# The first block's output projection as three fp32r products, with the low parts of two weight tiles made by GpSimd

## The chip, the cores and the metric

The program runs on one NeuronCore of a Trainium2 chip. The metric is the time of one execution on the device, in microseconds. The times here are the kernel's own: 1169.44 us is the median of three runs (1168.6 to 1170.05). A profile of one further execution gives the rows below.

## The reference, cut to what matters

Two stacks of two layers each work on 256 tokens of width 1024. Of a layer of the first stack, this is what lies around the change:

```python
merged = (gates[:, :, 0] * (y_ret.astype(x.dtype) @ p_ret[l])
          + gates[:, :, 1] * (y_fox.astype(x.dtype) @ p_fox[l])
          + gates[:, :, 2] * (y_rwkv.astype(x.dtype) @ p_rwkv[l]))
x = x + merged @ w_out[l]
h = _rmsnorm(x, ffn_norm[l])
gu = h @ w_gate_up[l]
g, u = jnp.split(gu, 2, axis=-1)
x = x + (jax.nn.silu(g) * u) @ w_down[l]
```

The change is in `merged @ w_out[l]`: a 256x1024 by 1024x1024 product in float32, once in each of the two layers of the first stack. The second stack has its own output projection, which is not touched.

## The kernel before, in words

Five engines run five programs written out by hand, which meet in semaphores (`Signal`). There is no scheduler: on each engine the order is that of the code. Activations lie transposed, features over the 128 partitions and 256 tokens along the free axis. Weights come as tiles of 128x2048 float32 (1 MB) into a ring of six slots. SyncE issues these loads in a fixed order, each after the wait that frees its slot. `SLOT1` says which slot tile n of a layer uses; tiles 26 to 29 are the four tiles q = 0 to 3 of `w_out`, 256 of its rows each.

A product that is to be exact enough is made in one of two ways. Either TensorE gets the float32 tiles as they are, and the trace then shows two MATMUL rows for each matmul of the program, or weight and activation are split: a high part, rounded to fp32r by a ScalarE copy (`ACT.Copy`), and a low part, the difference, by VectorE; the helper `passes` then gives three fp32r products, high by high, high by low and low by high, which add up in PSUM. The input projections (`group`, `fill`) and the FFN (`gate_up`, `down`) go the second way, the branch products (`merge`) and the output projection (`project`) the first.

The stretch around the change, once in a layer:

- `fill` finishes the input projection. TensorE solves the second half of the RWKV recurrence (`rt_chunk_terms`, `rt_state`, `rt_output`) and does blocks 0 to 3 of `merge` in between. ScalarE copies the results out of PSUM, VectorE makes the state (`state`, `state_step`).
- VectorE normalises the last output (`centre`, `head_sums`), GpSimd makes the inverse root (`inverse_root`), and VectorE ends with `normed(1)` and `finished(1)`, four operations of 128x256. TensorE meanwhile does merge blocks 4 to 6, then turns that output (`y_transposes`, after `y_ready`), and goes on with blocks 7 to 11.
- VectorE's `merged(n)` multiplies block n by its gate and adds it up: one operation that reads PSUM, then one with both inputs in SBUF. The last four write `mT`, the merged activations. Block n of `merge` waits for `merged(n - 4)`, since they share a bank.
- `project` runs over two pairs of tiles (q0 = 0, then 2), inside over the 8 output blocks m (bank m), inside that over the tiles of the pair and k = 0, 1: 64 matmuls of 128x256. In the second half each block m releases VectorE, which adds it to x.
- `ffn` starts. VectorE has to have made the low parts of the first gate and up tiles and of the normalised x. The loads of the second iteration's tiles wait for `wo_half` (first half of `project`) and `wo` (its end).

GpSimd does nothing else in this stretch than the `inverse_root` calls.

## Time and profile before

| | |
|---|---|
| median of three runs | 1169.44 us |
| the profiled execution | 1169.03 us |
| its span | 1167.2 us |
| granted TensorE clock, mean | 0.998 |
| ScalarE and VectorE, share of the span | 43%, 64% |
| GpSimd, share of the span | 5% |
| DMA, mean | 161 GB/s |

The span runs from the first to the last record of the profile; the time of the execution is 1.83 us longer. Busy time is given for each engine apart: PE is TensorE's matmul side, PEld its weight loads, which overlap, DVE is VectorE, ACT ScalarE, POOL GpSimd and SP SyncE. The page's slices show TensorE busy nine tenths or more of nearly the whole span, and the granted clock in the top tenth in all of them.

### The profile page before, as it was taken

The numbers are of one execution on the slowest core, as the hardware profiler recorded it, in microseconds if no ns is written. First come the engines' busy times: TensorE is split into PE (matmuls) and PEld (weight loads), VectorE is DVE, ScalarE is ACT, GpSimd is POOL, SyncE is SP. The second block draws the span as 40 slices with busy tenths as digits, with TensorE's granted clock in tenths as the row PEclk, the third lists the DMA queues.
The fourth block names the chain that finished last, engine by engine and source line by source line (L and its number), as shares of the span: only waits on it lengthen the run. The fifth ranks groups of instructions, "written<-read, shape, count | busy, mean of one in ns | idle before, by whom it ended". The sixth has DMA issues, their size and how long they took to land. (4 is left out here: it accounts for less than half of the span.)

```text
span 1167.2 us, 21650 instructions
## 1 busy us (share of the span) xinstructions
PE 1136.5 (97%) x9272; PEld 1018.4 (87%) x9272; DVE 744.3 (64%) x1090; ACT 505.2 (43%) x716; POOL 55.5 (5%) x47
## 2 busy tenths in 40 slices
PE   5999999999999999999999999999999999999997
PEld 4789998899999998799998899999997777877776
DVE  5587665736665565787675556555667675567744
ACT  5355442234333344455442143333355655446642
POOL 1002000000000000011000000000002100030000
PEclk9999999999999999999999999999999999999999
DMA  9543334454454355443335345434436334353310
GB/s 350 224 161 109 122 111 161 188 201 159 182 216 174 152 195 188 147 142 109 120 106 227 124 187 217 197 147 195 180 139 227 108 109 181 112 219 132 130 65 37
DMA packets 27465, 188.15 MB, mean 161 GB/s; under 512 B 3456, under 2 KB 4352, under 8 KB 5504
## 3 DMA queue, kind: packets, MB, share of 16 engines
q1 hardware_dynamic: 25808, 175.89, 40.8%
q10 hardware_dynamic: 1440, 8.55, 1.9%
q0 software_dynamic: 144, 2.66, 0.6%
q8 instruction: 55, 0.90, 0.3%
q14 instruction: 18, 0.15, 0.0%
HBM read 181.84 MB, written 5.24 MB: 160 GB/s over the span
## 5 line engine op out<-in xcount | busy, mean ns | idle before, releaser
L650 PE MATMUL bank<-in_low,h_high 128*128 128x512 f32 x352 | 138.4, 393 | 0.0
L650 PE MATMUL bank<-in_high,h_high 128*128 128x512 f32 x288 | 117.2, 407 | 13.4 <-DVE in_low L1932 12.1
L1069 PE MATMUL bank<-h_high,gate_split 128*128 128x256 f32 x704 | 129.1, 281 | 0.2
L1069 PE MATMUL bank<-h_high,up_split 128*128 128x256 f32 x704 | 128.6, 280 | 0.0
L1085 PE MATMUL bank<-act_split,down_split 128*128 128x256 f32 x960 | 118.4, 283 | 0.0
L1085 PEld LDWEIGHTS bank<-act_split,down_split 128*128 128x128 f32 x960 | 116.6, 192 | 0.0
L675 PE MATMUL bank<-h_high,in_high 128*128 128x256 f32 x384 | 115.7, 301 | 0.5 <-DVE in_low L1806 0.5
L1357 ACT ACTIVATE in_high<-ring 128x2048 fp32r<-128x2048 f32 x47 | 89.6, 1910 | 55.3 <-PE bank L650 54.7
L650 PE MATMUL bank<-in_high,x_low 128*128 128x512 f32 x288 | 113.3, 393 | 0.0
L1069 PEld LDWEIGHTS bank<-h_high,gate_split 128*128 128x128 f32 x704 | 109.9, 189 | 0.9 <-DVE h_low L1748 0.6
L1069 PEld LDWEIGHTS bank<-h_high,up_split 128*128 128x128 f32 x704 | 109.8, 189 | 0.0
L675 PE MATMUL bank<-x_low,in_high 128*128 128x256 f32 x384 | 108.4, 282 | 0.0
L675 PE MATMUL bank<-h_high,in_low 128*128 128x256 f32 x384 | 108.3, 282 | 0.0
L1806 DVE TENSOR_TENSOR in_low<-ring,in_high 128x2048 fp32r<-128x2048 f32 x35 | 79.9, 2289 | 35.7 <-ACT in_high L1357 35.7
L1069 PE MATMUL bank<-h_low,up_split 128*128 128x256 f32 x352 | 99.2, 282 | 0.0
L1069 PE MATMUL bank<-h_low,gate_split 128*128 128x256 f32 x352 | 99.2, 282 | 0.0
L1564 ACT ACTIVATE gate_split<-ring 128x2048 fp32r<-128x2048 f32 x24 | 46.0, 1917 | 91.7 <-PE bank L1069 72.4
L650 PEld LDWEIGHTS bank<-in_high,h_high 128*128 128x128 f32 x288 | 54.6, 190 | 27.7 <-issue 14.7
L650 PEld LDWEIGHTS bank<-in_low,h_high 128*128 128x128 f32 x352 | 66.8, 190 | 13.4 <-issue 0.5
L675 PEld LDWEIGHTS bank<-h_high,in_high 128*128 128x128 f32 x384 | 73.1, 190 | 5.7 <-issue 1.4
L2226 DVE TENSOR_TENSOR down_split<-ring,down_split 128x2048 fp32r<-128x2048 f32 x20 | 45.9, 2293 | 50.0 <-ACT down_split L1564 50.0
L675 PEld LDWEIGHTS bank<-x_low,in_high 128*128 128x128 f32 x384 | 73.3, 191 | 0.1
(339 smaller groups left out, 2252.4 us busy)
## 6 DMA issues: line engine op xcount, KB each, us to landing
ring<-w_in_dram SPq DMA_DIRECT2D x72, 1024.0 KB, 4.9
ring<-w_gate_up_dram SPq DMA_DIRECT2D x44, 1024.0 KB, 7.4
ring<-w_down_dram SPq DMA_DIRECT2D x22, 1024.0 KB, 4.8
ring<-w_out_dram SPq DMA_DIRECT2D x16, 1024.0 KB, 6.0
ring<-p_all_dram SPq DMA_DIRECT2D x6, 1024.0 KB, 4.8
x_kept<-scratch ACTq DMA_DIRECT2D x4, 1024.0 KB, 4.6
x<-x_kept ACTq DMA_DIRECT2D x4, 1024.0 KB, 7.8
table<-tables_dram POOLq DMA_DIRECT2D x1, 2594.0 KB, 12.2
```

Source lines behind the costliest of these rows:

```text
L650: last = mm(bank[(n - n % 2 + t) % 4][:], a, b, start=c == 0 and i == 0, stop=c == KT - 1 and i == 2)
L675: last = mm(bank[g % 4][:, half * 256:(half + 1) * 256], a, b, start=k == 0 and i == 0, stop=k == KT - 1 and i == 2)
L1069: last = mm(bank[2 * half + part][:, f * S:(f + 1) * S], a, b, start=k == 0 and i == 0, stop=k == KT - 1 and i == 2)
L1085: last = mm(bank[4 + m // 2][:, m % 2 * S:(m % 2 + 1) * S], a, b, start=False, stop=end and m % 2 == 1 and k == 1 and i == 2)
L1357: f(in_high[n % 2][:], ring[:, n % 4, :].rearrange("p (k n) -> p k n", k=KT), ACT.Copy).then_inc(done.sem, 1)
L1564: f(w_split[part if pair is None else pair][:, 0, :], ring[:, 3 * half + part, :], ACT.Copy).then_inc(w_hi[part].sem, 1)
L1806: tt(in_low[n % 4][:], ring[:, n % 4, :].rearrange("p (k n) -> p k n", k=KT), in_high[n % 2][:].bitcast(F32), ALU.subtract).then_inc(low.s ...
L2226: tt(w[:, 1, :], ring[:, 3 * half + part, :], w[:, 0, :].bitcast(F32), ALU.subtract)\
```

## The change

Each of the 64 products of `project` becomes three in fp32r. For that, the four tiles of `w_out` and the merged activations are split.

- ScalarE makes the high parts of the weights (`out_high`): tile 0 in two halves, between the copies of the recurrence; tile 1 after `gate_tanh(l, 2)`; tile 2 after `y_copy`; tile 3 after the last merge block. It also makes the high parts of the merged activations, two 128-row groups at a time (`merged_high`).
- GpSimd makes the low parts of tiles 0 and 1, two operations of 128x1024 each (its `out_low`). Tile 0 stands before the last `inverse_root` of the layer's recurrence, tile 1 right after it.
- VectorE makes the low parts of tiles 2 and 3 and of the merged activations, behind `merged(9)` and `merged(11)`.
- The high parts lie in parts of `scratch` and in `yT`, the low parts over the tile in its ring slot, and those of the activations over `mT`.
- `project` takes the first half's blocks in the order 3 to 7, 0, 1, 2.
- The tiles of `w_out` go to slots 5, 4, 3, 2 in place of 2, 3, 4, 5. Tile 0 may then be loaded one group earlier. Of the six FFN tiles that follow, the first down tile and the second gate tile wait for the end of `project` and no longer for its middle; the second up tile and second down tile wait for the middle, but stand behind those two in SyncE's queue.
- Eight semaphores of the second stack are shared with earlier ones to make room for the new ones.

```diff
@@ -132,7 +132,7 @@
 BRANCHES = [1, 0, 2]
-SLOT1 = [n % 4 for n in range(23)] + [3, 0, 1] + [2, 3, 4, 5]
+SLOT1 = [n % 4 for n in range(23)] + [3, 0, 1] + [5, 4, 3, 2]
 SLOT2 = [n % 4 for n in range(G2)] + [1, 2, 3, 5]
@@ -192,6 +192,7 @@
         vec = sb("vec", [P, N_VEC1])
+        yT_at = -(-nc.sbuf_base // 32) * 32
         yT = sb("yT", [P, 3, 2, S])
@@ -248,6 +249,12 @@
         in_low = [nc.alloc_sbuf_tensor_at(f"in_low{i}", [P, KT, 256], F32R, offset=ring_at + 8192 * i) for i in range(4)]
+        wo_high = [nc.alloc_sbuf_tensor_at(f"out_high{q}", [P, 2, D], F32R, offset=o)
+                   for q, o in enumerate((scratch_at + 4 * 12288, scratch_at, scratch_at + 4 * 7168, yT_at))]
+        wo_low = [nc.alloc_sbuf_tensor_at(f"out_low{q}", [P, 2, D], F32R, offset=ring_at + 8192 * SLOT1[26 + q]) for q in range(4)]
+        mT_high = nc.alloc_sbuf_tensor_at("merged_high", [P, KT, S], F32R, offset=scratch_at + 4 * 5120)
+        mT_low = nc.alloc_sbuf_tensor_at("merged_low", [P, KT, S], F32R, offset=scratch_at + 4 * 2048)
 
@@ -397,6 +404,11 @@
         mg_out = sig("merge_out", 12)
+        mt_hi = sig("merged_high", 4)
+        mt_lo = sig("merged_low", 4)
+        wo_hi = sig("out_high", 5)
+        wo_lo_p = sig("out_low_pool", 4)
+        wo_lo_v = sig("out_low_vector", 2)
         wo_half = sig("wo_first_half", 1)
@@ -418,15 +430,15 @@
-        b_rot = sig("b_rot", 3)
+        b_rot = goes_on(rt_msk, 3)
...
@@ -560,7 +572,7 @@
                     load(ring_in, [g_full.after(l, 20 + i)], s, ring[:, s, :], tile(p_all[ll, b]))
-                for q, free in ((0, g_full.after(l, 23)), (3, g_full.after(l, 22)), (2, g_full.after(l, 23)), (1, mg.after(l, 4))):
+                for q, free in ((0, g_full.after(l, 22)), (1, g_full.after(l, 23)), (3, g_full.after(l, 23)), (2, mg.after(l, 4))):
                     s = SLOT1[26 + q]
@@ -574,8 +586,8 @@
 
-                ffn_loads(0, 0, [mg.after(l, 8), mg.after(l, 12), wo_half.after(l, 1)])
-                ffn_loads(1, 1, [wo_half.after(l, 1), wo.after(l, KT), wo.after(l, KT)])
+                ffn_loads(0, 0, [mg.after(l, 8), mg.after(l, 12), wo.after(l, KT)])
+                ffn_loads(1, 1, [wo.after(l, KT), wo_half.after(l, 1), wo_half.after(l, 1)])
                 with sp.Fori(0, FF_IT // 2 - 1) as j:
@@ -1036,20 +1048,21 @@
                 for q0 in (0, 2):
-                    for m in range(KT):
+                    order = [3, 4, 5, 6, 7, 0, 1, 2] if q0 == 0 else range(KT)
+                    for n, m in enumerate(order):
                         for q in (q0, q0 + 1):
-                            if m == 0:
-                                s = SLOT1[26 + q]
-                                pe.wait_ge(*ring_in[s].after(l, SLOT1[:26 + q].count(s) + 1))
-                            if q == 0 and m < 3:
-                                pe.wait_ge(*mg_out.after(l, 10 + m))
-                            w = ring[:, SLOT1[26 + q], :].rearrange("p (k n) -> p k n", k=2)
+                            if n == 0:
+                                pe.wait_ge(*(wo_lo_p.after(l, 2 * q + 2) if q < 2 else wo_lo_v.after(l, q - 1)))
+                                pe.wait_ge(*mt_lo.after(l, q + 1))
+                            if q == 0 and (m < 3 or n == 0):
+                                pe.wait_ge(*mg_out.after(l, 10 + m if m < 3 else 9))
                             for k in range(2):
-                                last = mm(bank[m][:, 0:S], w[:, k, m * P:(m + 1) * P], mT[:, 2 * q + k, :],
-                                          start=q == 0 and k == 0, stop=q == 3 and k == 1)
+                                w = [v[:, k, m * P:(m + 1) * P] for v in (wo_high[q], wo_low[q])]
+                                for i, (a, b) in enumerate(passes(w, (mT_high[:, 2 * q + k, :], mT_low[:, 2 * q + k, :]))):
+                                    last = mm(bank[m][:, 0:S], a, b, start=q == 0 and k == 0 and i == 0, stop=q == 3 and k == 1 and i == 2)
                         if q0 == 2:
                             last.then_inc(wo.sem, 1)
-                        elif m == KT - 1:
+                        elif n == KT - 1:
                             last.then_inc(wo_half.sem, 1)
@@ -1361,6 +1374,17 @@
 
+            def out_high(l, q, half=None):
+                s = SLOT1[26 + q]
+                act.wait_ge(*ring_in[s].after(l, SLOT1[:26 + q].count(s) + 1))
+                c = slice(0, 2) if half is None else slice(half, half + 1)
+                f(wo_high[q][:, c, :], ring[:, s, :].rearrange("p (k n) -> p k n", k=2)[:, c, :], ACT.Copy).then_inc(wo_hi.sem, 1)
+            def merged_high(l, f2):
+                act.wait_ge(*mg_out.after(l, 9 + f2))
+                f(mT_high[:, 2 * f2:2 * f2 + 2, :], mT[:, 2 * f2:2 * f2 + 2, :], ACT.Copy).then_inc(mt_hi.sem, 1)
             def group(l, g, split=True):
@@ -1543,10 +1567,14 @@
                     last.then_inc(rt_txc.sem, 1)
+                    if t == 1:
+                        out_high(l, 0, 0)
                     act.wait_ge(*rt_h.after(l, t + 1))
                     for c in range(2):
                         last = f(m_h[:, c], bank[4 + c][:, 0:P].rearrange("p (i v) -> p i v", i=2), ACT.Copy)
                     last.then_inc(rt_hc.sem, 1)
+                    if t == 1:
+                        out_high(l, 0, 1)
                     act.wait_ge(*rt_y.after(l, t + 1))
@@ -1554,7 +1582,15 @@
                 gate_tanh(l, 2)
+                out_high(l, 1)
                 y_copy(l, 1, y_tp, yT[:, 2], bank[4], y_T, 0.5)
+                out_high(l, 2)
+                merged_high(l, 0)
+                merged_high(l, 1)
+                act.wait_ge(*mg.after(l, 12))
+                out_high(l, 3)
+                merged_high(l, 2)
+                merged_high(l, 3)
 
@@ -2216,8 +2252,26 @@
 
-                for n in range(4, 12):
+                def merged_low(f2):
+                    dve.wait_ge(*mt_hi.after(l, f2 + 1))
+                    c = slice(2 * f2, 2 * f2 + 2)
+                    tt(mT_low[:, c, :], mT[:, c, :], mT_high[:, c, :].bitcast(F32), ALU.subtract).then_inc(mt_lo.sem, 1)
+                def out_low(q):
+                    dve.wait_ge(*wo_hi.after(l, q + 2))
+                    tt(wo_low[q][:], ring[:, SLOT1[26 + q], :].rearrange("p (k n) -> p k n", k=2), wo_high[q][:].bitcast(F32),
+                       ALU.subtract).then_inc(wo_lo_v.sem, 1)
+                for n in range(4, 10):
                     merged(n)
+                merged_low(0)
+                merged_low(1)
+                merged(10)
+                merged(11)
+                out_low(2)
+                merged_low(2)
+                out_low(3)
+                merged_low(3)
 
@@ -2441,9 +2495,19 @@
                 inverse_root(st[:, 40:48], st[:, 32:40], 1.0 / HD, 1e-5, ret_rstd)
+                def out_low(q, half, hi):
+                    pool.wait_ge(*wo_hi.after(l, hi))
+                    nc.gpsimd.tensor_tensor(wo_low[q][:, half], ring[:, SLOT1[26 + q], half * D:(half + 1) * D],
+                                            wo_high[q][:, half].bitcast(F32), ALU.subtract).then_inc(wo_lo_p.sem, 1)
                 for t in range(NT):
+                    if t == 1:
+                        out_low(0, 0, 1)
+                        out_low(0, 1, 2)
                     pool.wait_ge(*rt_ysq.after(l, t + 1))
                     inverse_root(st[:, 72 + 8 * t:76 + 8 * t], st[:, 88 + 8 * t:92 + 8 * t], 1.0 / HD, 64e-5, rt_yrs)
+                for half in range(2):
+                    out_low(1, half, 3)
                 norm(2 * l + 1)
```

How GpSimd's program reads around the last two `inverse_root` calls of a layer (each is a TENSOR_SCALAR and a TENSOR_TENSOR on `small`), before:

```order
L2424 TENSOR_SCALAR small<-small 128x4
L2426 TENSOR_TENSOR small<-small,table 128x4
L2424 TENSOR_SCALAR small<-small 128x4
L2426 TENSOR_TENSOR small<-small,table 128x4
L2424 TENSOR_SCALAR small<-small 128x2
```

And now, where `out_low_63` and `out_low_64` are the low parts of `w_out` tiles 0 and 1:

```order
L2478 TENSOR_SCALAR small<-small 128x4
L2480 TENSOR_TENSOR small<-small,table 128x4
L2500 TENSOR_TENSOR out_low_63<-ring,out_high_59 128x1024 x2
L2478 TENSOR_SCALAR small<-small 128x4
L2480 TENSOR_TENSOR small<-small,table 128x4
L2500 TENSOR_TENSOR out_low_64<-ring,out_high_60 128x1024 x2
L2478 TENSOR_SCALAR small<-small 128x2
```

Two pairs of long two-input operations have come in, one on each side of the inverse root that VectorE's `normed(1)` waits for.

VectorE's program from the end of the merge to the FFN's first low parts, before (each pair of rows is one `merged`):

```order
L2100 SCALAR_TENSOR_TENSOR scratch<-arena,bank 128x512
L2102 TENSOR_TENSOR scratch<-arena,scratch 128x512
L2100 SCALAR_TENSOR_TENSOR scratch<-arena,bank 128x512
L2102 TENSOR_TENSOR scratch<-arena,scratch 128x512
L2226 TENSOR_TENSOR gate_split<-ring,gate_split 128x2048
L2226 TENSOR_TENSOR up_split<-ring,up_split 128x2048
L2258 TENSOR_TENSOR x<-x,bank 128x256 x4
```

And now:

```order
L2136 SCALAR_TENSOR_TENSOR scratch<-arena,bank 128x512
L2138 TENSOR_TENSOR scratch<-arena,scratch 128x512
L2258 TENSOR_TENSOR merged_low<-scratch,merged_high 128x512 x2
L2136 SCALAR_TENSOR_TENSOR scratch<-arena,bank 128x512
L2138 TENSOR_TENSOR scratch<-arena,scratch 128x512
L2136 SCALAR_TENSOR_TENSOR scratch<-arena,bank 128x512
L2138 TENSOR_TENSOR scratch<-arena,scratch 128x512
L2262 TENSOR_TENSOR out_low_65<-ring,out_high_61 128x2048
L2258 TENSOR_TENSOR merged_low<-scratch,merged_high 128x512
L2262 TENSOR_TENSOR out_low_66<-ring,out_high_62 128x2048
L2258 TENSOR_TENSOR merged_low<-scratch,merged_high 128x512
L2280 TENSOR_TENSOR gate_split<-ring,gate_split 128x2048
```

Six operations stand between the old ones: two low parts of activations ahead of the last two `merged`, the other four behind them and ahead of the FFN's.

ScalarE's program from the recurrence's second half on (`scratch<-bank` are the copies `txc`, `hc` and `y` of the recurrence, `arena<-arena` is `gate_tanh`, `yT<-bank` is `y_copy`), before:

```order
L1544 ACTIVATE scratch<-bank 64x512 x2
L1548 ACTIVATE scratch<-bank 128x128 x2
L1552 ACTIVATE scratch<-bank 64x256 x2
L1392 ACTIVATE arena<-arena 128x2048
L1396 ACTIVATE yT<-bank 128x512
L1564 ACTIVATE gate_split<-ring 128x2048
```

And now:

```order
L1568 ACTIVATE scratch<-bank 64x512 x2
L1382 ACTIVATE out_high_59<-ring 128x1024
L1574 ACTIVATE scratch<-bank 128x128 x2
L1382 ACTIVATE out_high_59<-ring 128x1024
L1580 ACTIVATE scratch<-bank 64x256 x2
L1416 ACTIVATE arena<-arena 128x2048
L1382 ACTIVATE out_high_60<-ring 128x2048
L1420 ACTIVATE yT<-bank 128x512
L1382 ACTIVATE out_high_61<-ring 128x2048
L1386 ACTIVATE merged_high<-scratch 128x512 x2
L1382 ACTIVATE out_high_62<-ring 128x2048
L1386 ACTIVATE merged_high<-scratch 128x512 x2
```

The order of the old copies among themselves has stayed; nine new ones stand between and behind them.

## Rows read from the trace of the kernel before

**Rows 1.** The page's first part: busy time of each engine.

```profile
PE 1136.5 (97%) x9272; PEld 1018.4 (87%) x9272; DVE 744.3 (64%) x1090; ACT 505.2 (43%) x716; POOL 55.5 (5%) x47
```

**Rows 2.** Line L1048, first layer: min/median/max ns, first and last start.

```profile
L1048 PE MATMUL bank<-scratch,ring x128: 379/379/379, 224.4 to 251.8; 128*128 128x256 f32 x128
```

**Rows 3.** Windows, L1069 alone: stretch, length, PE and PEld busy (rows), clock, DMA.

```profile
266.12:271.79 5.67, 5.65 (x48) 5.65 (x48) 1.00 0.00 0
```

**Rows 4.** Timeline, 209 to 216 us: start, length, engine, line, idle before.

```profile
209.49 1.91 ACT L1392 ACTIVATE arena<-arena 128x2048 f32<-128x2048 f32 x1 [0.25 <-DVE arena L2082]
...
212.25 1.01 POOL L2426 TENSOR_TENSOR small<-small,table 128x4 f32<-128x4 f32 x1
213.29 0.42 DVE L2110 TENSOR_TENSOR scratch<-scratch,small 128x256 f32<-128x256 f32 x1 [0.99 <-POOL small L2426]
...
214.78 0.43 DVE L2120 TENSOR_TENSOR scratch<-scratch 128x256 f32<-128x256 f32 x1
...
215.36 0.60 PE L735 MATMUL bank<-table,scratch 128*128 128x128 f32 x4
```

**Rows 5.** Line L2456, GpSimd, in the window 901.9 to 905.3 us.

```profile
L2456 POOL TENSOR_TENSOR scratch<-scratch,table x1: 4147/4147/4147, 902.0 to 902.0; 128x1024 f32<-128x1024 f32 x1
```

**Rows 6.** The same line in the window 905.2 to 908.6 us.

```profile
L2456 POOL TENSOR_TENSOR scratch<-scratch,table x2: 2392/3270/4147, 902.0 to 906.1; 128x1024 f32<-128x1024 f32 x2
```

**Rows 7.** Timeline of VectorE, 901 to 908 us.

```profile
901.58 2.29 DVE L1782 TENSOR_TENSOR in_low<-ring,in_high 128x2048 fp32r<-128x2048 f32 x1
...
907.92 0.70 DVE L1852 TENSOR_SCALAR scratch<-scratch,stats 128x256 f32<-128x256 f32 x1
```

**Rows 8.** Line L1852, VectorE, 895 to 1000 us.

```profile
L1852 DVE TENSOR_SCALAR scratch<-scratch,stats x24: 342/351/704, 907.9 to 964.7; 128x256 f32<-128x256 f32 x24
```

**Rows 9.** Timeline, 56 to 60 us.

```profile
56.67 1.67 POOL L2426 TENSOR_TENSOR small<-small,table 128x8 f32<-128x8 f32 x1 [30.96 <-issue]
57.32 2.29 DVE L1806 TENSOR_TENSOR in_low<-ring,in_high 128x2048 fp32r<-128x2048 f32 x1 [0.64 <-ACT in_high L1357]
```

**Rows 10.** Timeline, 201 to 207 us.

```profile
201.86 0.45 ACT L1548 ACTIVATE scratch<-bank 128x128 f32<-128x128 f32 x2 [1.37 <-PE bank L978]
...
205.15 0.59 DVE L2172 TENSOR_TENSOR kept<-scratch,small 64x128 f32<-64x128 f32 x2
...
206.39 0.44 PE L1006 MATMUL bank<-kept,scratch 128*64 128x128 f32 x4
```

**Rows 11.** DMA issued from 198.2 to 198.3 us: count, KB, us to landing.

```profile
ring<-w_out_dram SPq DMA_DIRECT2D x1, 1024.0 KB, 7.0
```

**Rows 12.** Timeline, 215 to 252 us.

```profile
215.88 0.69 DVE L2102 TENSOR_TENSOR arena<-arena,scratch 128x512 f32<-128x512 f32 x1
...
224.43 27.79 PE L1048 MATMUL bank<-scratch,ring 128*128 128x256 f32 x128
...
225.43 0.69 DVE L2102 TENSOR_TENSOR scratch<-arena,scratch 128x512 f32<-128x512 f32 x1
```

**Rows 13.** Timeline, 259 to 266 us.

```profile
259.28 1.92 ACT L1564 ACTIVATE gate_split<-ring 128x2048 fp32r<-128x2048 f32 x1
...
263.44 0.42 DVE L1776 COPY root<-bank 128x256 f32<-128x256 f32 x1
...
265.23 1.08 PE L1095 MATMUL bank<-h_high,zeros 128*128 128x512 f32 x4
```

**Rows 14.** DMA issued from 235 to 240 us.

```profile
ring<-w_gate_up_dram SPq DMA_DIRECT2D x1, 1024.0 KB, 7.5
```

**Rows 15.** Timeline of TensorE, from its first matmul on, and its last group.

```profile
12.10 0.77 PE L650 MATMUL bank<-in_high,h_high 128*128 128x512 f32 x1 [12.10 <-DVE in_low L1932]
...
16.49 0.40 PE L650 MATMUL bank<-in_low,h_high 128*128 128x512 f32 x1
...
1156.66 2.75 PE L1319 MATMUL bank<-scratch,table 128*128 128x256 f32 x12
```

**Rows 16.** Windows after it: stretch, length, five engines busy, granted clock, DMA.

```profile
1163.50:1164.50 1.00, 0.00 (x0) 0.00 (x0) 0.72 (x2) 0.00 (x0) 0.00 (x0) 0.50 0.89 353
```

More of the change, by code:

```diff
@@ L420, in build @@
         b_lame = sig("b_act", 2)
-        b_rot = sig("b_rot", 3)
-        b_tp = sig("b_tp", 8)
-        b_qk = sig("b_qk", 8)
-        b_gT = sig("b_gate_turned", 3)
+        b_rot = goes_on(rt_msk, 3)
+        b_tp = goes_on(rt_p, 8)
+        b_qk = goes_on(rt_akc, 8)
+        b_gT = goes_on(rt_hc, 3)
         b_dss = sig("b_dss", 1)
         b_drs = sig("b_drs", 1)
-        b_eg = sig("b_eg", 4)
-        b_mix = sig("b_mix", 4)
-        b_mtp = sig("b_mtp", 4)
+        b_eg = goes_on(rt_yc, 4)
+        b_mix = goes_on(rt_pc, 4)
+        b_mtp = goes_on(rt_q, 4)
         b_mT = sig("b_mT", 4)
```

## The prediction

> **What bounds the kernel now.** I read the page's busy times first. TensorE is busy 1136.5 us of the 1167.2 us span [rows 1], so a change counts by what it does to TensorE's stream: the time its own instructions take, and the time for which it is made to wait. Then the line of the old products: in the first layer they start at 224.4 us, the 128th at 251.8 us [rows 2], and in the timeline the first stands at 224.43, behind the merge without a gap [rows 12]. The second layer repeats this stretch 429.0 us later, so each number below counts twice. Last I read the timeline around the merge, to find where TensorE waits, or nearly waits, for the engines that now get more work.
>
> The reader is to see one tight place there. The inverse root on GpSimd ends at 213.26, VectorE's `normed(1)` and `finished(1)` run from 213.29 to 215.21, and the transposes of their result start on TensorE at 215.36 [rows 4]. Merge blocks 4 to 6 just cover this chain. Whatever it loses, TensorE loses.
>
> **What is gained.** The old stream: 251.8 less 224.4 is 27.4 us for 127 steps, 0.216 us each, so 27.6 us for 128 rows [rows 2]. The new one: 64 products times 3 are 192 fp32r matmuls of 128x256, in the pattern that the FFN uses. There 48 of them start within 5.66 us [rows 3], 0.118 us each, so 192 take 22.6 us. The gain is 5.0 us. Each half of `project` also begins with waits and new operands, for which I take off 0.1, so 4.9 us in a layer, and as bounds 4.7 and 5.0.
>
> **What GpSimd's work costs, the port.** This decides the case. GpSimd's new operations read two inputs in SBUF, and so do the four VectorE operations of the tight chain. The trace shows what the two engines do to each other. A GpSimd operation of 128x1024 takes 2.39 us undisturbed, but 4.15 us when it starts at 902.0 [rows 5, 6] into a VectorE operation with two SBUF inputs, which ends at 903.87 [rows 7]: it ended at 906.11, 2.24 us after VectorE. It had waited for all of the other. The other way round, the second GpSimd operation ran from 906.11 to 908.50 [rows 6]. The VectorE operation that started into it at 907.92 took 0.70 us [rows 7], where its like have a median of 0.35 [rows 8]. It ended at 908.62, so it came to work at 908.27, which is 0.23 us before GpSimd's record ends. Here VectorE waited. From these rows a GpSimd operation that gets the port keeps it for 2.24 less 0.23, 2.0 us.
>
> The Trainium skill says the same on its page "SBUF — State Buffer", section "Who interferes with whom": a VectorE instruction with two SBUF inputs and a GpSimd instruction that reads SBUF exclude each other, and whichever comes first holds the shared ports for its whole instruction. This rule speaks against the change. The trace agrees for long operations. It does not for the whole length: a small inverse root of 1.67 us, begun at 56.67, did not hold up a VectorE operation begun 0.65 us later, which took its usual 2.29 [rows 9].
>
> Tile 0 first. ScalarE is idle from 200.49 to 201.86 [rows 10], and the first half's copy, about half of the 1.91 us that 128x2048 takes [rows 4], fits in. Tile 0's load can go out one group before 198.2; a load issued at 198.2 landed after 7.0 us [rows 11]. So GpSimd's first operation runs from about 201.5 to 203.9, where VectorE works with one SBUF input, and its second, after the copy behind 202.31, from 203.9 to 206.3, with the port free at about 206.1. The state step of VectorE with two SBUF inputs wants to start at 205.15 [rows 10] and waits 0.9 us. It ends at 206.6 in place of 205.74, and `rt_output`, which starts at 206.39 [rows 10], waits for it: 0.3 us, bounds 0 and 0.5.
>
> Tile 1 now. `gate_tanh` ends at 211.4 [rows 4], ScalarE's copy of tile 1 follows and ends at 213.3, just as GpSimd is done with the inverse root. VectorE's first operation of the chain has the port until 213.71. GpSimd's first operation gets it until 215.7, and VectorE's second starts then in place of 213.78: 1.94 us late. GpSimd's next operation asks while that one runs, gets the port when it ends, and the third of VectorE is late by another 1.94. The chain ends at 219.1 in place of 215.2. Should GpSimd come first instead, the sum is the same. TensorE has nothing in its order to put there: it waits 3.9 us at the transposes. Bounds: 3.6 if a hold is 0.15 shorter, 4.6 if it lasts as long as the record of 2.39.
>
> By the page "GPSIMD Engine Reference", section "Performance versus the Vector engine", 2048 elements of such an operation take 4.497 us. An estimate from it is 2.25 us for 1024, and the chain would lose 0.3 us less.
>
> **What lies hidden.** ScalarE's copy of tile 2 falls into its idle time after `y_copy`. The other added work sits between the merge and the projection. VectorE's eight merges end 1.36 us apart, from 216.57 on [rows 12], so the fifth, `merged(8)`, is done at 222.0 and `merged(9)` at 223.4. ScalarE's first high part of the activations is done at 222.7 and the second at 224.1. The low parts follow at 224.1 and 224.8, where TensorE wants them at 224.43 and, behind its first six products, at 225.1. That is 0.3 us of cover. Since TensorE and VectorE are late by the same amount in the tight chain, the cover stays. The last two merges come 1.4 us later than now, until 227.5 in place of 226.1; their banks, 1 and 2, stand last in the new order and are wanted 8.5 us into the projection, at 232.9. The first half's end at 235.7 asks for low parts of tiles 2 and 3 and of the rest of the activations, which VectorE has made by 233.5: two of 2.29 and two of 0.69 after 227.5. If this were 3 us later TensorE would wait.
>
> Four FFN loads are issued after the projection's end instead of two. The first is a down tile, the second is gate tile 1, and a second load of such a pair lands 7.5 us after issue [rows 14], so about 7.9 after the end. ScalarE begins to copy this tile at 259.28 [rows 13], 7.1 us after the end at 252.2. The copy comes 0.8 us late, and with it VectorE's copy of the root, done at 263.86 where TensorE needs it at 265.23 [rows 13]: 1.4 us of cover, 0.8 of it used. Cost nothing. The shared semaphores of the second stack order nothing in time.
>
> **The sum.** In a layer 4.9 gained, 0.3 and 3.9 lost: 0.7 us faster, 1.4 for both. The profiled execution took 1169.03 us, so 1167.6. It stands 0.4 us under the median of 1169.44, and the forecast for the median is 1168.0 us. With the bounds taken together a layer comes out between 1.4 faster (5.0, less 0 and 3.6) and 0.4 slower (4.7, less 0.5 and 4.6), so this case's own range is 1166.6 to 1170.3.
>
> **The rivals.** One: the ports don't hold VectorE up, or GpSimd gives way. Then all of 4.9 us stays, in both layers 9.8, and the time is 1159.6. For it speaks the undisturbed operation of [rows 9]. Against it, that GpSimd operation has 8 elements a partition to read and may have been done with reading, while the long one made VectorE wait [rows 7]. 14%.
>
> Two: only one of the two holds falls into the chain, because VectorE gets the port ahead of GpSimd's second operation until the chain is done. A layer then has 4.9 less 0.3 and 1.94, 2.7 us, and the time is 1164.1. Between VectorE's four operations there are gaps of 0.07 us, in which nothing keeps a waiting GpSimd out; this speaks against. 13%.
>
> Three, the slower one: the wait of 3.9 us costs TensorE its clock. After the last matmul, which ends at 1159.4 [rows 15], the granted clock is 0.50 from 1163.5 on [rows 16], that is 1.2 GHz, after at most 4.1 us of idleness. At the start the matmuls run at half pace from 12.10 until about 16.3 [rows 15], 4.2 us, which costs 2.1. If each wait has this behind it, 4.2 us come to 1168.0: 1172.2. The point from which it decides is an idle stretch a little longer than I forecast; with the upper bounds of the holds the time would be 1174.5. For it: nothing in this trace lies between gaps that keep the clock and that last one. Against: the gap is no longer than what the clock outlasted there. Both layers 14%, and one layer alone, 1170.1, another 8%.
>
> Four: the change doesn't shorten the stream, since TensorE waits for low parts at the projection's start or for the root in the FFN. Each has its cover above. I leave it inside the 51% of the main case.
>
> **How the numbers follow.** The measurement tells 0.2%, 2.3 us, from no change: faster is under 1167.1, slower over 1171.8. Of the main case's 51% I put 15 under 1167.1, since its range reaches to 1166.6 and the cheaper bounds are as likely as the dear ones. Faster: 15, 14 and 13 give 42%. Same: 36 of the main case, 8 from the clock falling once, make 44%. Slower: 14%. The range goes down to 1159.2, to take in the first rival, and up to 1172.5, which leaves out the worse half of the third.
>
> **What would show it.** The new products start 0.118 us apart and last 22.6 us. TensorE's largest new wait stands before the transposes, 3.5 to 4.3 us, released by VectorE. The third and second operations of the chain there have records or starts that are 2 us late, each beside a GpSimd operation of 128x1024. `rt_output` waits 0.3 us. `project` itself has no wait over 0.3 us. I am wrong if the four operations of the chain end 1.9 us after they begin, as now, while GpSimd runs (then rival one), if the clock in the merge is under 1.0 (rival three), or if TensorE waits in `project` or ahead of the FFN's `zeros` products.

## The result, and the profile after

The changed kernel takes 1170.86 us (median of 15 runs, 1170.58 to 1173.34), against 1169.10 for the kernel before in the same session (15 runs, 1168.33 to 1170.05). The ratio is 1.0019, with an interval of 1.0012 to 1.0026. So the change costs 1.8 us, where I had forecast that it would bring 1.4. The runs form two clusters: eleven between 1170.58 and 1171.26, with a mean granted clock of 0.995 or 0.996, and four between 1172.79 and 1173.34, with 0.994. The profiled run (1170.76, span 1169.0) is of the first cluster.

I read the busy times first. This row is the page's first part and answers to [rows 1]:

```profile
PE 1130.5 (97%) x9400; PEld 1017.4 (87%) x9400; DVE 768.0 (66%) x1102; ACT 525.0 (45%) x734; POOL 74.2 (6%) x55
```

TensorE is busy 6.0 us less, and yet the span is 1.8 us longer. So TensorE waits more, and the question is where. The new products, line L1062 from 228 to 252 us (min/median/max ns, first and last start):

```profile
L1062 PE MATMUL bank<-merged_high,out_high x64: 277/281/467, 228.6 to 251.2; 128*128 128x256 f32 x64
L1062 PE MATMUL bank<-merged_low,out_high x64: 281/281/288, 228.9 to 251.3; 128*128 128x256 f32 x64
L1062 PE MATMUL bank<-merged_high,out_low x64: 278/282/287, 229.0 to 251.4; 128*128 128x256 f32 x64
```

The 192 start within 22.8 us (228.6 to 251.4), where the 128 starts of before took 27.4 [rows 2]. But they begin at 228.6 instead of 224.4. The timeline of VectorE from 213 to 220 us (start, length, line, idle before) shows what came ahead:

```profile
213.50 2.62 DVE L2146 TENSOR_TENSOR scratch<-scratch,small 128x256 f32<-128x256 f32 x1 [0.99 <-POOL small L2480]
216.20 2.40 DVE L2148 TENSOR_TENSOR scratch<-scratch,vec 128x256 f32<-128x256 f32 x1
218.67 0.43 DVE L2153 TENSOR_TENSOR scratch<-scratch 128x256 f32<-128x256 f32 x1
219.17 0.42 DVE L2156 TENSOR_TENSOR scratch<-scratch 128x256 f32<-128x256 f32 x1
```

and that of GpSimd in the same stretch:

```profile
212.46 1.01 POOL L2480 TENSOR_TENSOR small<-small,table 128x4 f32<-128x4 f32 x1
213.49 4.83 POOL L2500 TENSOR_TENSOR out_low<-ring,out_high 128x1024 fp32r<-128x1024 f32 x2
```

These are `normed(1)` and `finished(1)`, which took 0.42 us an operation [rows 4]. The first two now have records of 2.62 and 2.40 us, each beside one of GpSimd's two operations on tile 1. The third and fourth, after GpSimd's end at 218.32, have their old length. The reader is to see that a stopped operation shows a long record here, not idle time before it. Then TensorE's timeline, of both layers (215 to 230 us, 640 to 662 us):

```profile
219.65 0.66 PE L747 MATMUL bank<-table,scratch 128*128 128x128 f32 x4 [3.74 <-DVE scratch L2156]
220.15 8.80 PE L1044 MATMUL bank<-yT,ring 128*128 128x256 f32 x40
228.59 0.47 PE L1062 MATMUL bank<-merged_high,out_high 128*128 128x256 f32 x1
...
648.86 1.11 PE L747 MATMUL bank<-table,scratch 128*128 128x128 f32 x4 [3.75 <-DVE scratch L2156]
649.76 11.20 PE L1044 MATMUL bank<-yT,ring 128*128 128x256 f32 x40
660.61 0.47 PE L1062 MATMUL bank<-merged_high,out_high 128*128 128x256 f32 x1
```

The waits are alike, 3.74 and 3.75 us. What follows them is not. The same 40 matmuls take 8.80 us in the first layer and 11.20 in the second. Windows of the second layer (stretch, length, busy PE, PEld, DVE, ACT, POOL, granted clock, DMA share, GB/s):

```profile
646.00:647.00 1.00, 0.00 (x0) 0.00 (x0) 1.00 (x1) 0.00 (x0) 1.00 (x1) 1.00 0.00 0
647.00:648.00 1.00, 0.00 (x0) 0.00 (x0) 0.92 (x2) 0.00 (x0) 0.52 (x1) 0.89 0.00 0
648.00:650.00 2.00, 1.14 (x5) 1.15 (x6) 1.85 (x4) 0.00 (x0) 0.00 (x0) 0.50 0.00 0
650.00:652.00 2.00, 2.00 (x6) 1.55 (x6) 1.93 (x4) 1.99 (x2) 0.00 (x0) 0.50 0.00 0
652.00:654.00 2.00, 2.00 (x6) 1.58 (x5) 1.40 (x3) 0.41 (x1) 0.00 (x0) 0.50 0.00 0
654.00:655.00 1.00, 1.00 (x5) 0.82 (x4) 0.80 (x2) 0.00 (x0) 0.00 (x0) 0.69 0.90 131
```

Within the wait the granted clock falls from 1.00 to 0.50, which is from 2.4 to 1.2 GHz, and it is back only after 654. From the transposes' start to the projection's are 8.94 us in the first layer and 11.75 in the second, so the fall costs 2.81 us. In the first layer the clock was 1.00 throughout.

The rest can be read from four marks in each layer: one merge step of VectorE that waits 7.40 us for TensorE in every kernel (W, at 201.20 before), the first transposes of the third branch (X), the projection's first product (Y), and the FFN's first `zeros` product (Z). Distances in us:

```text
                            W to X   X to Y   Y to Z
before, first layer          14.16     9.07    40.80
changed, first layer         18.54     8.94    36.35
changed, second layer        18.55    11.75    36.08
before, second layer         14.16     9.07    40.81
```

W to Z is 0.20 shorter in the first layer and 2.34 longer in the second. The remainder, from the start to W, between the layers, and behind the second Z, sums to -0.34 us (-0.09, +0.38 and -0.63). Together that is 1.8.

The first layer's Y to Z is 0.27 longer than the second's. One wait explains it. ScalarE, 258 to 263 us:

```profile
260.31 1.92 ACT L1600 ACTIVATE gate_split<-ring 128x2048 fp32r<-128x2048 f32 x1 [1.45 <-DMA ring<-w_gate_up_dram]
```

Before, this copy began at 259.28 without a wait [rows 13]. VectorE's copy of the root comes behind it, and TensorE's `zeros` wait for that.

### The profile page after: what moved, and what is told of

It is laid out like the page before. It is cut to its first block and busy times, and to the rows that moved or that the text cites. A ratio compares the mean times of both kernels' runs of the same rounds, so it can differ in the third digit from the quotient of the medians.

```text
span 1169.0 us, 21952 instructions
## 1 busy us (share of the span) xinstructions
PE 1130.5 (97%) x9400; PEld 1017.4 (87%) x9400; DVE 768.0 (66%) x1102; ACT 525.0 (45%) x734; POOL 74.2 (6%) x55
```

## The experiments

Nine kernels ran. The kernel before ran beside them and had medians of 1169.16 to 1169.29 us.

**Tile 1's low parts on VectorE, projection tile by tile.**

```diff
-                for q0 in (0, 2):
+                for q0, tiles in enumerate(((0,), (1,), (2, 3))):
...
-                        for q in (q0, q0 + 1):
+                        for q in tiles:
...
                 merged(11)
+                out_low(1)
                 out_low(2)
...
-                for half in range(2):
-                    out_low(1, half, 3)
```

> GpSimd makes the low parts of tile 0 alone. VectorE makes those of tile 1 behind its last merge step, and the projection runs through tile 0, then tile 1, then tiles 2 and 3, so that tile 1's low parts are wanted some 2.6 us later than now. Theory A (the two tile-1 operations of GpSimd stop VectorE's two short operations at 213.5 and 216.2, this delays TensorE's transposes by 3.7 us, and in a layer where the clock falls behind that delay another 2.4 us are lost): the transposes start near 215.5 again in both layers, the granted clock stays at 1.00 through the merge and the projection, and what is left is the gain of the projection of 4.7 less 0.4 for tile 0's stop and less 0.2 at the first zeros of the feed-forward part, which is 4.1 a layer: 1169.1 - 8.2 = 1160.9 us, between 1160.3 and 1162. Rival B (the delay has another cause, as the new order of loads or ScalarE's four copies of high parts, and GpSimd's second tile is innocent): the wait of about 3.7 us stays ahead of the transposes, and the time is that of the changed kernel or above, 1170 to 1172. Rival C (VectorE can't carry tile 1: TensorE then waits inside the projection for its low parts): the transposes start on time, but a gap of 1 to 3 us stands between the blocks of tile 0 and those of tile 1, 1163 to 1167.

Measured: 1160.72 us (5 runs, 1160.14 to 1161.18), ratio 0.9926, interval 0.9913 to 0.9940. VectorE's four operations in the timeline:

```profile
214.04 0.42 DVE L2146 TENSOR_TENSOR scratch<-scratch,small 128x256 f32<-128x256 f32 x1 [0.99 <-POOL small L2481]
214.54 0.43 DVE L2148 TENSOR_TENSOR scratch<-scratch,vec 128x256 f32<-128x256 f32 x1
215.04 0.42 DVE L2153 TENSOR_TENSOR scratch<-scratch 128x256 f32<-128x256 f32 x1
215.54 0.43 DVE L2156 TENSOR_TENSOR scratch<-scratch 128x256 f32<-128x256 f32 x1
```

The transposes start at 216.29 and not near 215.5, but W is later by 0.45 too, at 201.65. W to X is 14.64 us, and the clock is 1.00 until the kernel's last microseconds. X to Y (8.89) and Y to Z (36.24 and 36.10) are as short as in the changed kernel, so VectorE carries tile 1 without making TensorE wait. Theory A holds, and rivals B and C fall.

**Tile 1's operations of GpSimd cut to 8 columns.** The kernel leaves out the rest of tile 1's low parts; the projection's matmuls stay as many.

```diff
-                                w = [v[:, k, m * P:(m + 1) * P] for v in (wo_high[q], wo_low[q])]
+                                w = [v[:, k, m * P:(m + 1) * P] for v in (wo_high[q], wo_low[0 if q == 1 else q])]
...
-                    out_low(1, half, 3)
+                    pool.wait_ge(*wo_hi.after(l, 3))
+                    nc.gpsimd.tensor_tensor(wo_low[1][:, half, 0:8], ...)
```

> Leaves out most of tile 1's low parts: GpSimd's two operations on them take 8 columns in place of 1024, and the projection's second product of tile 1 reads tile 0's low parts in their place. Nothing else changes: same loads, same high parts on ScalarE, same order of blocks, same waits. Theory A (VectorE is stopped by the length of GpSimd's two operations): VectorE's two operations at 213.5 and 216.2 take 0.42 each again, the transposes start near 215.6, the clock stays up, and the time is 1169.1 - 2 x 4.1 = 1160.9, between 1160.3 and 1162. Rival B (loads or ScalarE's copies cause the delay): at least half of the 3.7 us stays, 1166 or more.

Measured: 1159.54 us (5 runs, 1159.31 to 1160.18), ratio 0.9919 (0.9906 to 0.9933). W to X is 14.63 in both layers. Loads, ScalarE's copies and the order of blocks are those of the changed kernel, so the 18.54 less 14.63, 3.91 us, are due to the length of these two GpSimd operations alone. That the time is 1.2 us under the version above lies ahead of W, which stands at 200.51 here and at 201.65 there. I have no cause for that, and since the runs of one kernel also differ by about a microsecond I draw nothing from it.

**TensorE kept at work in the wait.** The changed kernel with 14 matmuls ahead of the transposes, whose results nobody reads.

```diff
                 merge(l, 1, range(3))
+                for _ in range(14):
+                    mm(bank[7][:], zeros[:], h_high[:, 0:2, :]..., start=True, stop=True)
                 y_transposes(l, 2, w_y, y_ready, 2, y_tp, bank[4])
```

> The changed kernel with 14 more matmuls per layer (zeros by 512 columns of h_high into bank 7, read by nobody; about 3.2 us together at the full clock) in TensorE's program ahead of the transposes that wait. They lie within the wait of 3.7 us, so they cost nothing themselves. Theory A (the clock's fall in layer 2 is due to TensorE's idle time of 3.75 us, and is worth 2.4 us): the granted clock is 1.00 through the merge in both layers, the transposes start no later, and the profiled time is 2.4 lower than the 1170.8 of the changed kernel, 1168.4 (1167.9 to 1169.0); the few runs near 1173 are gone, too. Rival D (the fall has nothing to do with that idle time, and comes from elsewhere, or costs nothing): 1170.6 to 1171.5, with stretches of half clock at the same place. Rival E (the filler delays the transposes or holds bank 7): above 1171.5, with the transposes later than 219.7.

Measured: 1167.62 us (11 runs, 1167.25 to 1168.29, all with a mean clock of 0.998 or 0.999), ratio 0.9989 (0.9980 to 0.9998). The timeline of TensorE:

```profile
215.46 3.56 PE L1201 MATMUL bank<-h_high,zeros 128*128 128x512 f32 x14
219.62 0.66 PE L747 MATMUL bank<-table,scratch 128*128 128x128 f32 x4 [0.60 <-DVE scratch L2158]
...
648.45 0.66 PE L747 MATMUL bank<-table,scratch 128*128 128x128 f32 x4 [0.59 <-DVE scratch L2158]
648.95 8.80 PE L1044 MATMUL bank<-yT,ring 128*128 128x256 f32 x40
```

W to X is 18.62, so VectorE's stops are all there. Only TensorE's idleness is gone, and with it the fall: X to Y is 8.94 in both layers, and the second cluster of runs doesn't appear. The time falls by 3.2 us against the changed kernel. 2.8 of it is the fall of the second layer. 0.3 is the first layer's wait at `zeros`, which is absent here (Y to Z is 36.09): the gate tile landed earlier, and ScalarE's copy waited 0.21 us in place of 1.45. Why it landed earlier isn't known. I had expected 2.4 for the fall. Useless work on TensorE made the kernel faster, theory A holds, and rivals D and E fall.

**GpSimd's operations on tile 1 in quarters.**

```diff
-                    out_low(1, half, 3)
+                    pool.wait_ge(*wo_hi.after(l, 3))
+                    for c in range(2):
+                        last = nc.gpsimd.tensor_tensor(wo_low[1][:, half, c * 512:c * 512 + 512], ...)
+                    last.then_inc(wo_lo_p.sem, 1)
```

> Each of GpSimd's two tile-1 operations is cut in two of 512 columns, the same work in four operations of about 1.2 us each. Theory A (VectorE is stopped until the GpSimd operation that is under way ends, and gets its turn between two of them): VectorE's short operations get in at each of the ends, three of them are stopped for about 1.05 us each, and the transposes start near 218.9 in place of 219.65, 0.6 to 0.8 us a layer less; with a gap of 3.0 us in place of 3.7 the clock may hold in both layers, so 1166.9 to 1169.5. Rival F (GpSimd keeps what it holds from one operation to the next when they stand back to back): VectorE is stopped for one long stretch of some 4.8 us, and the transposes start near 218.5 or later with one operation of VectorE of over 4 us in the trace. Rival B (another cause than GpSimd's length): no change, 1170.6 to 1171.2.

Measured: 1170.05 us (11 runs, 1167.95 to 1172.86), ratio 1.0009 (0.9999 to 1.0019). The median lies outside both ranges. VectorE, and GpSimd beside it:

```profile
213.27 1.54 DVE L2146 TENSOR_TENSOR scratch<-scratch,small 128x256 f32<-128x256 f32 x1 [0.99 <-POOL small L2480]
214.88 1.33 DVE L2148 TENSOR_TENSOR scratch<-scratch,vec 128x256 f32<-128x256 f32 x1
216.28 1.33 DVE L2153 TENSOR_TENSOR scratch<-scratch 128x256 f32<-128x256 f32 x1
217.68 1.33 DVE L2156 TENSOR_TENSOR scratch<-scratch 128x256 f32<-128x256 f32 x1
...
213.25 5.47 POOL L2512 TENSOR_TENSOR out_low<-ring,out_high 128x512 fp32r<-128x512 f32 x4
```

The two engines take turns, as theory A has it, one operation of VectorE behind each of GpSimd. Rival F falls. But all four of VectorE's operations are stopped, by 1.12 and three times 0.91 us, not three of them. W to X is 18.18, which saves 0.36 us a layer and not 0.6 to 0.8. The wait of TensorE is 3.38 us, and in the profiled run (1168.33) the clock still falls in the second layer, for a shorter time: X to Y is 10.32 there, 1.38 more than at full clock. The runs lie in clusters again, from 1168 to 1172.9: five at 0.997 up to 1168.80, six at 0.994 to 0.996 from 1170.05 on. I take the second group for runs with longer or more falls; no profile was taken of one, so that isn't shown.

**GpSimd's tile 1 behind the tight chain.**

```diff
+                pool.wait_ge(*y_ready.after(l, 2))
                 for half in range(2):
                     out_low(1, half, 3)
```

> The changed kernel with one more wait on GpSimd: its two tile-1 operations start only when VectorE has finished the third branch's last operation, so they no longer stop the four short operations ahead of the transposes. They then run beside the merge. Theory A (what is stopped is whatever VectorE operation of two tensors comes next, and VectorE has no slack in the merge, where it is busy 4.7 of 5 us): the transposes start near 215.6, two merge operations of VectorE take about 2.6 us in place of 0.7, TensorE runs dry inside the merge or ahead of the projection, the projection starts near 228.5 again, and the time is that of the changed kernel within 1 us when the clock falls, 1168 to 1171. Rival H (the merge absorbs the stops, since TensorE bounds it): the projection starts near 225, 1160.5 to 1163.

Measured: 1165.64 us (6 runs, 1164.96 to 1166.58), ratio 0.9969 (0.9957 to 0.9981). It fits neither range. VectorE and GpSimd, and then TensorE, in the merge:

```profile
216.39 0.68 DVE L2136 SCALAR_TENSOR_TENSOR scratch<-arena,bank 128x512 f32<-128x512 f32 x1
217.14 2.32 DVE L2138 TENSOR_TENSOR arena<-arena,scratch 128x512 f32<-128x512 f32 x1
219.39 0.68 DVE L2136 SCALAR_TENSOR_TENSOR scratch<-arena,bank 128x512 f32<-128x512 f32 x1
220.13 2.09 DVE L2138 TENSOR_TENSOR arena<-arena,scratch 128x512 f32<-128x512 f32 x1
222.15 0.67 DVE L2136 SCALAR_TENSOR_TENSOR scratch<-arena,bank 128x512 f32<-128x512 f32 x1
...
216.55 5.13 POOL L2500 TENSOR_TENSOR out_low<-ring,out_high 128x1024 fp32r<-128x1024 f32 x2 [2.04 <-DVE scratch L2156]
```

```profile
219.61 1.96 PE L1044 MATMUL bank<-yT,ring 128*128 128x256 f32 x8 [0.48 <-DVE arena L2138]
222.28 5.45 PE L1044 MATMUL bank<-yT,ring 128*128 128x256 f32 x24 [0.71 <-DVE arena L2138]
228.40 0.36 PE L1062 MATMUL bank<-merged_high,out_high 128*128 128x256 f32 x1 [0.67 <-issue]
```

Only L2138, with both inputs in SBUF, is stopped, by 1.6 and 1.4 us. L2136, which reads a bank, runs at its 0.68 beside GpSimd. The Trainium skill has it so on its page "SBUF — State Buffer", section "Who interferes with whom": a VectorE instruction with at most one SBUF input doesn't contend with GpSimd outside the modes that use two ports. The rows agree: in this stretch a hold costs something only while an operation with two SBUF inputs is due. X to Y is 11.60 us in place of 8.88, so 2.7 of the 3.0 us still reach TensorE. They reach it in three pauses of 0.48, 0.71 and 0.67 us by the rows (at each the starts lose a little more, since the records of matmuls overlap where nothing waits), and the clock stays at 1.00. I had tied the price to a fall of the clock. Without one the same GpSimd work costs 4.9 us over both layers, against the tile-by-tile version, and 6.1 against the one with tile 1 cut.

**Shorter idle stretches.** The filler kernel with 6 and with 10 matmuls in place of 14.

```diff
-                for _ in range(14):
+                for _ in range(6):
```

> The kernel with filler matmuls, with 6 in place of 14 of them per layer: TensorE works 1.3 us of the wait of 3.7 us and idles for 2.4. Theory A (an idle stretch of TensorE of 3.4 to 3.75 us is followed by a fall of the clock in some layers and runs): with 2.4 us the clock holds at 1.00 in both layers, 1167.6 as with 14. If the clock falls behind 2.4 us as well: groups of runs near 1170 and 1172 again, and a stretch at 0.50 near 648. Rival D (a fall has nothing to do with the idle stretch): a stretch at 0.50 whatever the number of fillers.

> The kernel with filler matmuls, with 10 of them per layer: an idle stretch of about 1.5 us is left ahead of the transposes, between the 0.60 (14 fillers: the clock held in 11 of 11 runs) and the 2.40 (6 fillers: it fell in both layers of the profiled run, and in 8 of 10 runs the time is 1169.7 or more). If a stretch of 1.5 us is short enough: 1167.6 in all runs, the clock at 1.00 until the end. If not: groups near 1168.9 and 1170.2, and stretches at 0.50 behind the transposes.

Measured with 6: 1170.17 us (10 runs, 1167.92 to 1170.64), ratio 1.0005 (0.9996 to 1.0015). Two runs lie at 1167.92 and 1168.44 with a mean clock of 0.998 or more, eight from 1169.70 to 1170.64 with 0.996 or 0.997. The profiled one is of the eight. Its transposes and its windows in the first layer (columns as above):

```profile
218.99 0.66 PE L747 MATMUL bank<-table,scratch 128*128 128x128 f32 x4 [2.40 <-DVE scratch L2158]
```

```profile
218.00:219.00 1.00, 0.01 (x1) 0.01 (x1) 0.91 (x3) 0.00 (x0) 0.00 (x0) 1.00 0.00 0
219.00:220.00 1.00, 1.00 (x6) 0.97 (x7) 0.92 (x2) 0.31 (x1) 0.00 (x0) 0.87 0.00 0
220.00:221.00 1.00, 1.00 (x4) 0.72 (x3) 0.93 (x3) 1.00 (x2) 0.00 (x0) 0.50 0.03 8
221.00:222.00 1.00, 1.00 (x4) 0.81 (x3) 1.00 (x2) 1.00 (x1) 0.00 (x0) 0.50 0.00 0
222.00:223.00 1.00, 1.00 (x3) 0.80 (x3) 0.93 (x3) 0.08 (x1) 0.00 (x0) 0.50 0.00 0
223.00:224.00 1.00, 1.00 (x6) 0.82 (x5) 0.93 (x3) 0.00 (x0) 0.00 (x0) 0.92 0.79 98
```

After 2.40 us of idleness the clock falls in both layers, for a shorter time each. In the rows it falls between 219 and 220, when the transposes have already begun (218.99), so here it comes behind the wait and not in it. X to Y is 10.63 and 10.62, 1.7 us more than at full clock. So my forecast that the clock holds with 2.4 us was wrong.

Measured with 10: 1168.04 us (10 runs, 1167.56 to 1170.38), ratio 0.9995 (0.9985 to 1.0004). In the profile the waits are 1.50 and 1.49, the clock 1.00, X to Y 8.94. Eight runs lie from 1167.56 to 1168.37, two at 1170.37 and 1170.38. These two have a mean clock of 0.998 like the others, so what held them up isn't known.

**Tile 0's operations cut as well.** The kernel leaves out most of the low parts of both tiles.

```diff
-                                w = [v[:, k, m * P:(m + 1) * P] for v in (wo_high[q], wo_low[q])]
+                                w = [v[:, k, m * P:(m + 1) * P] for v in (wo_high[q], wo_low[q] if q > 1 else wo_high[q])]
...
-                    nc.gpsimd.tensor_tensor(wo_low[q][:, half], ...)
+                    nc.gpsimd.tensor_tensor(wo_low[q][:, half, 0:8], ...)
```

> Leaves out most of the low parts of tiles 0 and 1: all four of GpSimd's operations take 8 columns, and the projection's second product of these tiles reads their high parts in place of the low ones. Theory A (tile 0's first operation stops one operation of VectorE at 205 for 1.2 us, which costs 0.4 a layer at the third recurrence's output step): that operation takes 0.59 us again, TensorE's instruction near 206.5 loses its wait, and the time is 1159.5 - 0.8 = 1158.7 (1158.3 to 1159.1). Rival I (tile 0's stop has cover and costs nothing): 1159.5, the time of the version with tile 1's operations cut alone.

Measured: 1159.23 us (5 runs, 1158.92 to 1159.95), ratio 0.9917 (0.9904 to 0.9931). By the median it is 0.3 us under the version with tile 1 cut, where 0.8 was expected; it fits neither range. The traces show why. VectorE's state step in the changed kernel:

```profile
205.06 1.62 DVE L2208 TENSOR_TENSOR kept<-scratch,small 64x128 f32<-64x128 f32 x2
```

and here:

```profile
204.72 0.59 DVE L2208 TENSOR_TENSOR kept<-scratch,small 64x128 f32<-64x128 f32 x2
```

W to X is 14.16 in both layers, as before the change, so tile 0's stop costs 0.47 us a layer there. But Y to Z is longer than with tile 1 alone cut: 36.67 against 36.40 in the first layer and 36.28 against 36.10 in the second. Only 0.19 and 0.28 us are left at Z. In the first layer the gate tile is the reason: ScalarE's copy waits for it and starts at 255.84 (255.79 with tile 1 alone cut), although the projection begins 0.21 us earlier. The second layer's 0.18 has no wait beside it that I found.

**SyncE's loads in another order,** on top of the tile-by-tile version: two tiles of the second FFN block as soon as the projection's first half is done, then the gate tile, then the down tile.

```diff
-                ffn_loads(0, 0, [mg.after(l, 8), mg.after(l, 12), wo.after(l, KT)])
-                ffn_loads(1, 1, [wo.after(l, KT), wo_half.after(l, 1), wo_half.after(l, 1)])
+                for b, free, wt, it, part in ((0, mg.after(l, 8), w_gate_up, 0, 0), (1, mg.after(l, 12), w_gate_up, 0, 1),
+                                              (4, wo_half.after(l, 1), w_gate_up, 1, 1), (5, wo_half.after(l, 1), w_down, 1, 0),
+                                              (3, wo.after(l, KT), w_gate_up, 1, 0), (2, wo.after(l, KT), w_down, 0, 0)):
+                    load(ring_in, [free], b, ring[:, b, :], block_tile(wt, ll, it, part))
```

> The tile-by-tile version with SyncE's last four loads of the projection in another order: the two that wait only for the projection's first half come first, then the gate tile of the second feed-forward block, then the down tile of the first. Theory A (the first zeros of the feed-forward part are late by 0.24 us because ScalarE waits 1.36 us for a gate tile that lands 8 us after its issue, behind a down tile and among three other loads): the gate tile lands 1 us or more earlier, ScalarE's copy no longer waits for it, and the time falls by 0.2 to 0.3 a layer, 1160.7 - 0.5 = 1160.2 (1159.9 to 1160.5). Rival G (the gate tile isn't what sets the zeros' start, or the loads issued earlier slow something else): 1160.7 or above.

Measured: 1160.59 us (5 runs, 1159.72 to 1160.84), ratio 0.9926 (0.9912 to 0.9939), against 1160.72: no difference that these runs can show. The trace shows the step itself:

```profile
254.59 1.92 ACT L1602 ACTIVATE gate_split<-ring 128x2048 fp32r<-128x2048 f32 x1
```

The copy no longer waits (1.36 us in the tile-by-tile version), and Y to Z is 36.09 in the first layer in place of 36.24. In the second it was 36.10 already and stays (36.08). So the wait exists in one layer only, and is worth 0.15 us here.

## Why the prediction was wrong

**The gain.** 4.9 us a layer forecast. Y to Z is shorter by 4.73 where nothing waits, X to Y by 0.13: 4.86. Right. My cover for the root fell short: from the projection's end to the gate tile's copy were 8.6 us in the first layer, where I had 7.9 and before it was 7.1. The copy was late by 1.6 and not by 0.8, against a cover of 1.4, and this cost 0.27, where I had put nothing.

**Tile 0.** 0.3 us forecast, within 0 to 0.5. Measured 0.47 at the transposes. Right in kind, at the upper end.

**The two holds in the tight chain.** 3.9 us forecast, 3.91 measured. Right, also in the form: GpSimd and VectorE take turns. In detail the first operation of the chain, L2146 at 213.50, was stopped and not the second; the case in which GpSimd comes first, with the same sum. Rivals one and two fall.

**What lies hidden.** TensorE waits nowhere inside `project`; only its first two products start 0.31 us apart, where the others start 0.12 apart. The cover of 0.3 us held. In the first layer, where the clock didn't fall, the sum is 4.86 less 0.47, 3.91 and 0.27: 0.2 us faster, as measured (W to Z, 64.03 to 63.83). I had 0.7.

**The failed step is "the gap is no longer than what the clock outlasted there".** In rival three I took 4.1 us of idleness behind the last matmul as a length that the clock survives, and gave the fall in one layer 8% and in both 14%. The changed kernel shows a fall in the second layer after 3.75 us; the shorter waits of 3.38 and 2.40 us were followed by falls as well, while 3.74 in the first layer was not. "The point from which it decides is an idle stretch a little longer than I forecast" is therefore refuted. The price was too small as well: I had 2.1 us from the kernel's start, and the fall took 2.81. So the term that was missing, or rather left to a rival, is this fall. It came in every run of the changed kernel at least once, by the mean clocks (0.994 to 0.996, where the kernel before has 0.998 or 0.999), and in four of fifteen with a lower mean clock and 2 us more, which I take for a second, shorter fall; no profile was taken of these four, so that isn't shown. With the gap filled, the time is 1167.62, 0.4 us from my forecast of 1168.0, but that is in part luck: each layer is 0.4 us faster there and not 0.7 (W to Z 63.65 and 63.63), and the other 0.7 us come from outside the two stretches, where I had forecast nothing. Of the cases that I listed, "one layer alone, 1170.1" is the one that came, given 8%.

My reasoning had a fault that can be named. One row at the kernel's end gave an upper bound of the time to a fall at that place. I used it as a lower bound of the time for which idleness is safe.

**What stays open.** Why the fall comes in one layer and not in the other after equal waits, and why it comes in both after the shorter wait of 2.40 us. And why the stretch behind the second Z is 0.6 us shorter than before, in the changed kernel and in the variants read (472.2 to 472.4 us against 472.9), and that between the layers 0.2 to 0.5 longer.

## What to carry to other kernels

Work given to an idle GpSimd isn't free where VectorE has short operations with two SBUF inputs on the critical path. Here operations of 0.3 to 0.7 us were stopped until the long GpSimd operation under way was done, while GpSimd's operations of 8 columns made the first of them longer by 0.05 us at most. So put such work where VectorE reads PSUM or has slack, or make it later by running the consumer tile by tile, as here (1160.7 us, 0.74% less than before). If a change makes a saturated TensorE wait for microseconds, read the granted clock behind the wait, and price the wait and the fall apart. A filler that keeps TensorE at work through the wait tells the two apart.

## What the runs showed of the hardware that I had not expected

- An idle stretch of TensorE of 2.40 us was followed by half clock in both layers of one profile, 3.38 and 3.75 us in one layer of two, 1.50, 0.71 and 0.60 in none. After each of these falls the clock came back while TensorE was busy. The falls cost 1.7 us each (behind 2.40), 1.38 (behind 3.38) and 2.81 (behind 3.75), so a longer wait didn't always cost more.
- Two GpSimd operations back to back let one VectorE operation in between: cut in four they stopped four VectorE operations by 0.91 to 1.12 us each, as two they stopped two by 2.20 and 1.97.
- The windows of the kernel before show a granted clock of 1.00 from 12 to 16 us, though the same matmuls of 512 columns start 0.43 us apart there and 0.23 from 16.5 on. So at the kernel's start the level has to be read from the spacing of the matmuls.
